# Two matmuls that share a rounded weight, joined into one 512-column matmul, in the MLP and the queries of a two-stack kernel

## The chip, the cores and the metric

The kernel runs on one core of one Trainium2 chip. The metric is the device time of one execution in microseconds. The kernel before takes 3531.47 us, the median of three runs (3530.13 to 3538.19).

## The reference

The reference runs two transformer stacks, two layers each, over 256 tokens of width 1024, in float32. What the change touches are the MLP of each layer of the first stack and the query projection of the expert layer of each layer of the second.

```python
# first stack, each layer l (x: 256 x 1024, mlp_up: 1024 x 4096, mlp_down: 4096 x 1024)
h2 = rms_norm(x, mlp_norm_g[l])
x = x + jnp.square(jax.nn.relu(h2 @ mlp_up[l])) @ mlp_down[l]

# second stack, peer_ffn (w_q: 1024 x 2048)
q = (h @ w_q).astype(f32).reshape(bsz, s, PEER_HEADS, 2, PEER_DKEY // 2)
```

## The kernel before

The kernel is written by hand for each engine: every engine has its own program in a fixed order, and semaphores hold them together. Activations are kept transposed, 128 features on the partitions and the 256 tokens (S) along the free side. A product with a weight matrix is cut into tiles of 128 output features. A tile has one or more units; a unit is eight chunks (KD) of 128x128 weights, 1024 numbers per partition, which SP's queue loads into one of eight slots of a ring (RING).

**Split products.** TensorE multiplies float32 in full in two passes, and numbers rounded to a shorter float (F32R) in one. The kernel splits both operands into a rounded part ("high") and the rounded rest ("low") and adds three products: low weight by high input, high weight by low input and high weight by high input. stream_split does this on TensorE: for each unit three passes of eight 256-column matmuls into the first half of one PSUM bank. Up tiles from number RAW = 3 on (29 of 32 in each layer), all eight down tiles (four units each) and query tiles 3 to 15 go through it. The first three up and query tiles are plain float32, computed before the norm is known (raw_tiles, raw_out).

**The split of a weight.** ScalarE copies a unit from the ring to weight_high (weights_high, line 1961, four slots, three units ahead); VectorE then puts the ring's value minus the high part back into the ring's slot (weights_low, line 2988, two units ahead). Behind every second unit of the MLP VectorE does one add_mod (lines 2966 and 2969, 128x1024), a step of the second stack's modulation vectors. Loads for these steps share SP's queue with the weights.

**An up tile.** TensorE finishes tile j; ScalarE evacuates it with Relu (evac, line 1726), squares it (line 2255) and copies it to up_high (line 2257), each waiting for the one before; VectorE takes the rest, up_low (line 3391). ScalarE's order is: weights_high for tile j, evacuation of j, Square, Copy. VectorE's is: weights_low for tile j, rest of j. In layer 1, VectorE also makes the angles of the second stack's rotary tables before tiles 8 and 14 and their cosines before 12 and 18 (ANGLES, COSINES), and ScalarE their sines before tiles 10 and 16 (SINES). TensorE does 16 small matmuls for modulation sums before tile 22 (UP_SUM, line 1011), and others between down tiles.

**Down and queries.** A down tile is evacuated by ScalarE and added to the residual by VectorE (line 3024); ScalarE squares the result for the next norm. Unit u of the first down tile waits for eight up_low. A query tile is only evacuated, to pq_t. At the first up and query tile, TensorE waits chunk by chunk for hidden_high (ScalarE, line 1948) and for its rest, h_low or second_low (VectorE, split_hidden, line 3001).

Tiles rotate over three banks (BANKS): a tile waits until the one three before it is evacuated.

Of the kernel before, what the change touches and what calls it, by code (L numbers as in the profile page):

```python
# [19 lines left out]
F32 = mybir.dt.float32  # L20
# [155 lines left out]
def two_stacks(nc, io, out):  # L176
    ctx = ExitStack()
    with ctx:
# [14 lines left out]
        def rounded(name, over, first, shape):  # L193

            t = nc.alloc_sbuf_tensor_at(name, shape, F32R, offset=address[over] + 4 * first)
            return t[(slice(None),) * len(shape)]

        arena = sb("arena", [P, 32768])
        ring = sb("ring", [P, RING, 1024])
# [21 lines left out]
        less = rounded("less", "less_plain", 0, [P, P])  # L221
        h_low = rounded("h_low", "hT", 0, [P, KD, S])
        t_high, t_low = rounded("t_high", "hT", 0, [P, KD, S]), rounded("t_low", "ring", 6 * 1024, [P, KD, S])

        PB = [ctx.enter_context(nc.psum_tensor(f"bank{i}", [P, 512], F32)) for i in range(8)]

        def C(name):
# [294 lines left out]
        weight_low = rounded("weight_low", "ring", 0, [P, RING, 1024])  # L522
        hidden_high = rounded("hidden_high", "arena", 25856, [P, KD, S])
        first_weight_high = rounded("first_weight_high", "arena", 0, [P, HIGH, 1024])
        first_high, first_low = rounded("first_high", "uT", 0, [P, KD, S]), rounded("first_low", "arena", 30112, [P, KD, S])
        second_low = rounded("second_low", "arena", 27904, [P, KD, S])
# [15 lines left out]

        up_high = rounded("up_high", "arena", 0, [P, 32, S])
        up_low = rounded("up_low", "arena", 13568, [P, 32, S])

# [233 lines left out]
        gains_m, gains_f = small[:, 24:32], small[:, 32:40]  # L779
        behind_raw = [tiles[label][0] for label in [("conv", RAW)] + [("pq", l, RAW) for l in range(DEPTH)]]  # L780

# [37 lines left out]
        def _(eng):  # L819
# [31 lines left out]

            def stream_split(label, high, low, ready=(None, None), unit_ready=None):

                t, first, count, n = tiles[label]
                assert first == used[0], (label, first, used[0])
                if t + 1 > BANKS:
                    eng.wait_ge(sem("evac"), t + 1 - BANKS)
                for u in range(count):
                    m, k = used[0], units[used[0]][0][1]
                    used[0] += 1  # L860
                    if unit_ready:
                        eng.wait_ge(sem(unit_ready), pe.next(unit_ready, k))
                    eng.wait_ge(sem("weight_low"), split_at[m] + 1)
                    wh = high_of(m)[:, 0:k * P].rearrange("p (k n) -> p k n", n=P)
                    wl = weight_low[:, slot_of[m], 0:k * P].rearrange("p (k n) -> p k n", n=P)
                    for part, (w, x) in enumerate(((wl, high), (wh, low), (wh, high))):
# [448 lines left out]
            def experts(l):  # L1315

                for j in range(RAW, 16):
                    stream_split(("pq", l, j), hidden_high, second_low,
                                 ("hidden_high", "hidden_split") if j == RAW else (None, None))
                for j in range(4):  # L1320
# [285 lines left out]
            for l in range(DEPTH):  # L1606
# [30 lines left out]
                for j in range(RAW, DFF // P):  # L1637
                    if j == UP_SUM:
                        mod_sums(l, 2)
                    stream_split(("up", l, j), hidden_high, h_low,  # L1640
                                 ("hidden_high", "hidden_split") if j == RAW else (None, None))
                def down(m):
                    if m in DOWN_SUMS:
                        mod_sums(l, DOWN_SUMS[m])
                    stream_split(("down", l, m), up_high, up_low, unit_ready=None if m else "up_split")

# [58 lines left out]
        def _(eng):  # L1705
# [259 lines left out]
            def to_residual(name, l, buf, raw=None, gains=None, squares=square_of):  # L1965
# [6 lines left out]
                for m in range(KD):  # L1972
# [4 lines left out]
                    if act.reused("res_add", 4):  # L1977
                        eng.wait_ge(sem("res_add"), act.freed("res_add", 4))
                    evac((name, l, m), buf[:, m % 4, :])
                    if m:  # L1980
# [232 lines left out]
            for l in range(DEPTH):  # L2213
# [32 lines left out]
                for j in range(DFF // P):  # L2246
# [291 lines left out]
        def _(eng):  # L2538
# [78 lines left out]
            def shifted_later(g):  # L2617

                scaled(hT, g, "h_scaled")
                dve.next("h_ready", KD)  # L2620

            def two_norms():
# [390 lines left out]
            def residual(name, l, buf, gain=None):  # L3013
                for m in range(KD):
# [4 lines left out]
                    if name == "down" and m == KD - 1:  # L3019
                        for i in range(MOD_STEPS - 2, MOD_STEPS):  # L3020
                            add_mod(l, i)
                    copied_out((name, l, m))
                    if gain is None:
# [318 lines left out]
            for l in range(DEPTH):  # L3342
# [39 lines left out]
                for j in range(DFF // P):  # L3382
# [15 lines left out]
            for l in range(DEPTH):  # L3398
# [63 lines left out]
```

## Time and profile before

| | before |
|---|---|
| median of three runs | 3531.47 us |
| the three runs | 3530.13, 3531.47, 3538.19 us |
| span of the profiled execution | 3528.6 us |
| TensorE matmul busy | 3419.6 us, 97% |
| TensorE weight load busy | 3075.1 us, 87% |
| VectorE busy | 2454.6 us, 70% |
| ScalarE busy | 1629.3 us, 46% |
| mean granted TensorE clock | 0.988 of full |

The profile comes from an execution whose span, first to last instruction, is 3528.6 us; the time of a run holds some 3 us around that (3531.47 - 3528.6 = 2.9 us). In the rows, PE is TensorE's matmul, PEld its weight load, DVE VectorE, ACT ScalarE. A matmul's duration (283 ns for 256 columns) is longer than the step from one start to the next, because they overlap: the rate is read from start times. L870 is the matmul of stream_split. Names of tensors are the program's; "arena" and "ring" are large buffers that hold many things in turn.

### The profile page before, as it was taken

The numbers are of one execution on the slowest core, as the hardware profiler recorded it, in microseconds if no ns is written. First come the engines' busy times: TensorE is split into PE (matmuls) and PEld (weight loads), VectorE is DVE, ScalarE is ACT, GpSimd is POOL, SyncE is SP. The second block draws the span as 40 slices with busy tenths as digits, with TensorE's granted clock in tenths as the row PEclk, the third lists the DMA queues.
The fourth block names the chain that finished last, engine by engine and source line by source line (L and its number), as shares of the span: only waits on it lengthen the run. The fifth ranks groups of instructions, "written<-read, shape, count | busy, mean of one in ns | idle before, by whom it ended". The sixth has DMA issues, their size and how long they took to land.

```text
span 3528.6 us, 69418 instructions
## 1 busy us (share of the span) xinstructions
PE 3419.6 (97%) x24762; PEld 3075.1 (87%) x24762; DVE 2454.6 (70%) x5088; ACT 1629.3 (46%) x3273; POOL 323.4 (9%) x438
## 2 busy tenths in 40 slices
PE   8999999999999999999999999999899999999998
PEld 7879899988888998889888888888789888888887
DVE  6734456665435756547998888887447998888887
ACT  4143355434434643145555555554345555555554
POOL 0212000020210000000550000000000550000000
PEclk9999999999999999999999999999999999999999
DMA  7633478764336875134348778777254348787775
GB/s 219 182 90 97 116 220 262 229 189 120 84 95 184 262 236 129 49 104 144 92 122 195 193 191 192 190 192 172 63 147 143 91 128 193 190 194 191 192 192 134
DMA packets 644022, 565.20 MB, mean 160 GB/s; under 512 B 62027, under 2 KB 589402, under 8 KB 643546
## 3 DMA queue, kind: packets, MB, share of 16 engines
q1 hardware_dynamic: 638564, 542.16, 58.4%
q0 software_dynamic: 4960, 19.93, 1.7%
q8 instruction: 149, 2.44, 0.3%
q14 instruction: 71, 0.58, 0.1%
q10 hardware_dynamic: 278, 0.08, 0.0%
HBM read 550.52 MB, written 9.44 MB: 159 GB/s over the span
## 4 chain that ended last, share of the span: by engine, by line
PE 90%; DVE 4%; ACT 2%; DMA 1%; issue 1%; POOL 0%; SPq 0%; DVEq 0%; ACTq 0%; POOLq 0%
PE bank L1433 16%; PE bank L870 14%; PE bank L848 14%; PE bank L1453 7%; PE bank L1447 7%; PE bank L1450 7%; PE bank L891 4%; PE bank L1410 3%; PE bank L1385 3%; PE bank L844 2%; PE bank L1395 2%; PE bank L1364 1%; PE bank L1244 1%; PE bank L915 1%; PE bank L959 1%
## 5 line engine op out<-in xcount | busy, mean ns | idle before, releaser
L1433 PE MATMUL bank<-t_high,u_parts 128*128 128x256 f32 x3072 | 431.7, 283 | 5.1 <-DVE u_parts L3278 5.1
L1433 PEld LDWEIGHTS bank<-t_high,u_parts 128*128 128x128 f32 x3072 | 398.4, 188 | 43.3 <-issue 22.4
L3299 DVE TENSOR_TENSOR v_low<-ring,v_high 128x512 fp32r<-128x512 f32 x512 | 337.0, 689 | 62.9 <-ACT v_high L2167 38.3
L1453 PE MATMUL bank<-v_low,w_high 128*128 128x512 f32 x1024 | 323.2, 397 | 0.0
L1447 PE MATMUL bank<-v_high,w_high 128*128 128x512 f32 x1024 | 318.6, 392 | 0.0
L2167 ACT ACTIVATE v_high<-ring 128x512 fp32r<-128x512 f32 x512 | 299.3, 620 | 41.5 <-PE bank L1453 41.5
L1450 PE MATMUL bank<-v_high,w_low 128*128 128x512 f32 x1024 | 315.9, 390 | 0.0
L2370 POOL TENSOR_SCALAR uT<-cst,selT 128x128 f32<-128x128 f32 x256 | 188.2, 744 | 1352.2 <-ACT selT L2092 1347.8
L1726 ACT ACTIVATE arena<-bank 128x256 f32<-128x256 f32 (+1 forms) x270 | 103.8, 387 | 446.4 <-PE bank L848 249.6
L2155 ACT ACTIVATE u_parts<-bank 128x512 fp32r<-128x512 f32 x384 | 217.7, 593 | 194.8 <-DVE bank L3271 193.1
L848 PE MATMUL bank<-hT,ring 128*128 128x256 f32 (+2 forms) x1232 | 283.1, 387 | 9.4 <-DVE hT L2587 5.9
L848 PEld LDWEIGHTS bank<-hT,ring 128*128 128x128 f32 (+2 forms) x1232 | 231.3, 190 | 52.9 <-issue 17.7
L848 PE MATMUL bank<-arena,ring 128*128 128x256 f32 (+2 forms) x1168 | 270.2, 384 | 5.3 <-DVE arena L3010 3.0
L3278 DVE TENSOR_TENSOR u_parts<-bank,u_parts 128x512 fp32r<-128x512 f32 x384 | 246.9, 685 | 12.8 <-ACT u_parts L2155 0.6
L3271 DVE STREAM_TRANSPOSE bank<-ring 128x512 f32<-128x512 f32 x384 | 251.8, 701 | 1.0 <-DMA ring<-in_peer_u 1.0
L848 PEld LDWEIGHTS bank<-arena,ring 128*128 128x128 f32 (+2 forms) x1168 | 217.1, 190 | 40.1 <-DVE arena L3010 3.9
L2178 ACT ACTIVATE w_high<-tab 128x256 fp32r<-128x256 f32 x256 | 107.1, 418 | 280.4 <-DVE tab L3293 280.4
L1450 PEld LDWEIGHTS bank<-v_high,w_low 128*128 128x128 f32 x1024 | 192.3, 188 | 43.1
L1453 PEld LDWEIGHTS bank<-v_low,w_high 128*128 128x128 f32 x1024 | 192.1, 188 | 40.7 <-DVE v_low L3299 0.2
L1433 PE MATMUL bank<-t_low,u_parts 128*128 128x256 f32 x1536 | 214.2, 281 | 0.4
L2988 DVE TENSOR_TENSOR weight_low<-ring,weight_high 128x1024 fp32r<-128x1024 f32 x148 | 179.8, 1221 | 46.4 <-ACT weight_high L1961 45.4
L1447 PEld LDWEIGHTS bank<-v_high,w_high 128*128 128x128 f32 x1024 | 179.1, 188 | 29.7
(455 smaller groups left out, 6434.0 us busy)
## 6 DMA issues: line engine op xcount, KB each, us to landing
ring<-in_peer_v SPq DMA_DIRECT2D x256, 512.0 KB, 4.6
ring<-in_peer_u SPq DMA_DIRECT2D x768, 128.0 KB, 4.3
ring<-in_w_in SPq DMA_DIRECT2D x128, 512.0 KB, 4.0
ring<-in_mlp_up SPq DMA_DIRECT2D x64, 512.0 KB, 4.3
uT<-in_mod_w SPq DMA_DIRECT2D x64, 512.0 KB, 4.9
ring<-in_mlp_down SPq DMA_DIRECT2D x64, 512.0 KB, 4.1
ring<-in_peer_u SPq DMA_DIRECT2D x64, 512.0 KB, 3.8
arena<-in_mod_w POOLq DMA_DIRECT2D x32, 512.0 KB, 4.9
```

Source lines behind the costliest of these rows:

```text
L848: ins = eng.matmul(ps[0:n, 0:width], wv[:, i, :], moving(u * 8 + i), start=(u == 0 and i == 0), stop=(u == count - 1 and i == k - 1))
L870: ins = eng.matmul(PB[t % BANKS][:, 0:S], w[:, i, :], x[:, u * 8 + i, :], start=(u == 0 and part == 0 and i == 0), stop=(u == count - 1 an ...
L1433: ins = eng.matmul(PB[6 + b][:, 0:S], u_parts[:, part, k * P:k * P + P], moving[:, k, :], start=(n == 0), stop=(n == len(products) - 1))
L1447: eng.matmul(PB[2 * tt + q][:, :], w_high[:, b, t], v_high[:, d], start=first, stop=False)
L1450: eng.matmul(PB[2 * tt + q][:, :], w_low[:, b, t], v_high[:, d], start=False, stop=False)
L1453: ins = eng.matmul(PB[2 * tt + q][:, :], w_high[:, b, t], v_low[:, j % 4, d], start=False, stop=last)
L2155: eng.activation(u_parts[:, 0, d], PB[4 + q][:, :], ACT.Copy).then_inc(sem("uH_ready"), 1)
L2167: eng.activation(v_high[:, d], ring[:, 2 + j % 4, d], ACT.Copy).then_inc(sem("vH_ready"), 1)
L2370: ins = ts_(one_p[:, b, j, :], C("iota"), selT[:, 1, at], None, ALU.is_equal)
L3271: eng.transpose(PB[4 + q][:, :].rearrange("p (k e j) -> p k e j", e=QUADS, j=32), blocks_of(f, q)).then_inc(sem("u_turned"), 1)
L3278: tt_(u_parts[:, 1, d], PB[4 + q][:, :], u_parts[:, 0, d].bitcast(F32), ALU.subtract).then_inc(sem("uL_ready"), 1)
L3299: tt_(v_low[:, j % 4, d], ring[:, 2 + j % 4, d], v_high[:, d].bitcast(F32), ALU.subtract).then_inc(sem("vL_ready"), 1)
```

## The change

For a weight chunk, the passes high by low and high by high have the same stationary operand. They become one matmul of 512 columns: its moving operand is two strips of 256 columns, the high and the low input, some way apart in memory (pairs), and its result goes to the two halves of a bank (halves). Low by high stays a 256-column matmul and adds to the first half. In the first unit of a tile the first pair comes before everything else, since it opens the bank.

The two halves have to be added. ScalarE copies the second half to the destination (half_out) and VectorE adds the first to it (both_out). evac now counts up on VectorE for these tiles. For up, Relu can only follow the addition: it is a ScalarE operation of its own, with a wait, before Square. VectorE takes the rest of tile j-1 (up_rest) after both_out of tile j. The gates and the first projections keep their three passes.

```diff
+        def pairs(one, other):
+            apart = other.offset - one.offset
+            return lambda i: bass.AP(one.tensor, (one if apart > 0 else other).offset + S * i,
+                                     [list(one.ap[0]), [abs(apart), 2], [1, S]])
...
+            def pair_products(ps, bank, wh, wl, high, pair, at, k, ready, first, last):
+
+                def from_pair(i):
+                    if ready[1]:
+                        eng.wait_ge(sem(ready[1]), pe.next(ready[1]))
+                    return eng.matmul(halves(bank), wh[:, i, :], pair(at + i), start=(first and i == 0),
+                                      stop=(last and i == k - 1))
+
+                for i in range(k):
+                    if ready[0]:
+                        eng.wait_ge(sem(ready[0]), pe.next(ready[0]))
+                    if first and i == 0:
+                        from_pair(0)
+                    eng.matmul(ps[:, 0:S], wl[:, i, :], high[:, at + i, :], start=False, stop=False)
+                for i in range(1 if first else 0, k):
+                    ins = from_pair(i)
+                return ins
...
+            def half_out(label, dest):
+                t = by_vector(label) - 1
+                eng.wait_ge(sem("unit_done"), last_unit(label))
+                eng.activation(dest, PB[t % BANKS][:, S:2 * S], ACT.Copy).then_inc(sem("half_out"), 1)
...
-                        evac(("pq", l, j), pq_t[:, j, :])
+                        half_out(("pq", l, j), pq_t[:, j, :])
...
-                        evac(("up", l, j), up_t[:, j, :], ACT.Relu)
+                        half_out(("up", l, j), up_t[:, j, :])
                     eng.wait_ge(sem("evac"), tiles[("up", l, j)][0] + 1)
+                    if j >= RAW:
+                        eng.activation(up_t[:, j, :], up_t[:, j, :], ACT.Relu).then_inc(sem("act_step"), 1)
+                        eng.wait_ge(sem("act_step"), act.next("act_step"))
                     eng.activation(up_t[:, j, :], up_t[:, j, :], ACT.Square).then_inc(sem("act_step"), 1)
...
+            def both_out(label, dest):
+                eng.wait_ge(sem("half_out"), dve.next("half_out"))
+                tt_(dest, dest, PB[tiles[label][0] % BANKS][:, 0:S], ALU.add).then_inc(sem("evac"), 1)
...
                     if j >= RAW:
                         weights_low(("up", l, j))
-                    eng.wait_ge(sem("up_high"), dve.next("up_high"))
-                    tt_(up_low[:, j, :], up_t[:, j, :], up_high[:, j, :].bitcast(F32), ALU.subtract).then_inc(sem("up_split"), 1)
+                        both_out(("up", l, j), up_t[:, j, :])
+                    if j:
+                        up_rest(j - 1)
+                up_rest(DFF // P - 1)
...
                 for j in range(RAW, 16):
                     weights_low(("pq", l, j))
+                    both_out(("pq", l, j), pq_t[:, j, :])
```

## Rows read from the trace of the kernel before

**Rows 1.** The page: busy us and instructions by engine; the chain's shares by engine.
```profile
PE 3419.6 (97%) x24762; PEld 3075.1 (87%) x24762; DVE 2454.6 (70%) x5088; ACT 1629.3 (46%) x3273; POOL 323.4 (9%) x438
...
PE 90%; DVE 4%; ACT 2%; DMA 1%; issue 1%; POOL 0%; SPq 0%; DVEq 0%; ACTq 0%; POOLq 0%
```
**Rows 2.** Stretches: us, busy PE, PEld, DVE, ACT, POOL; granted clock, DMA share, GB/s.
```profile
482.00:569.00 87.00, 87.00 (x722) 86.77 (x721) 65.41 (x84) 65.10 (x121) 0.00 (x0) 1.00 0.88 265
...
1558.00:1566.00 8.00, 7.76 (x32) 6.09 (x31) 7.86 (x18) 4.55 (x12) 0.00 (x0) 0.79 0.29 83
```
**Rows 3.** Groups of matmuls by line and shape: count, busy us, mean ns.
```profile
L870 PE MATMUL bank<-up_low,weight_high 128*128 128x256 f32 x512 | 71.9, 283 | 0.0
...
L870 PE MATMUL bank<-h_low,weight_high 128*128 128x256 f32 x464 | 65.1, 283 | 0.0
```
**Rows 4.** Timeline, TensorE, first down unit of layer 0: start us, us, what, count.
```profile
569.07 1.12 PE L870 MATMUL bank<-up_high,weight_low 128*128 128x256 f32 x8
```
**Rows 5.** Timeline, TensorE, two stretches of the expert stage's 512-column matmuls.
```profile
1827.48 0.63 PE L1447 MATMUL bank<-v_high,w_high 128*128 128x512 f32 x2
...
1829.77 0.63 PE L1453 MATMUL bank<-v_low,w_high 128*128 128x512 f32 x2
...
1834.09 0.63 PE L1447 MATMUL bank<-v_high,w_high 128*128 128x512 f32 x2
...
1838.28 0.63 PE L1447 MATMUL bank<-v_high,w_high 128*128 128x512 f32 x2
```
**Rows 6.** Timeline, ScalarE, first up tiles of layer 0.
```profile
488.19 0.36 ACT L1726 ACTIVATE arena<-bank 128x256 f32<-128x256 f32 x1
488.58 0.42 ACT L2255 ACTIVATE arena<-arena 128x256 f32<-128x256 f32 x1
489.03 0.42 ACT L2257 ACTIVATE up_high<-arena 128x256 fp32r<-128x256 f32 x1
489.36 1.04 ACT L1961 ACTIVATE weight_high<-ring 128x1024 fp32r<-128x1024 f32 x1
490.31 0.36 ACT L1726 ACTIVATE arena<-bank 128x256 f32<-128x256 f32 x1
```
**Rows 7.** Groups on VectorE with a bank as operand.
```profile
L2815 DVE TENSOR_TENSOR arena<-arena,bank 128x256 f32<-128x256 f32 x48 | 20.2, 421 | 19.8 <-PE bank L1250 10.3 <-PE bank L1244 8.1
```
**Rows 8.** Timeline, VectorE, layer 1's up part: angles, a lesser weight, an add_mod.
```profile
1147.66 0.35 DVE L2554 TENSOR_SCALAR arena<-wT,cst 128x256 f32<-128x256 f32 x1
...
1150.40 1.23 DVE L2988 TENSOR_TENSOR weight_low<-ring,weight_high 128x1024 fp32r<-128x1024 f32 x1
1151.55 1.28 DVE L2969 SCALAR_TENSOR_TENSOR arena<-uT,cond,arena 128x1024 f32<-128x1024 f32 x1
1152.74 0.42 DVE L3391 TENSOR_TENSOR up_low<-arena,up_high 128x256 fp32r<-128x256 f32 x1
```
**Rows 9.** Timeline, TensorE, last pass of the first split up tile, layer 0.
```profile
485.69 1.12 PE L870 MATMUL bank<-hidden_high,weight_high 128*128 128x256 f32 x8
```
**Rows 10.** Timeline, TensorE, modulation sums before up tile 22.
```profile
538.49 1.84 PE L1011 MATMUL bank<-cst,arena 128*128 128x1 f32 x16
```
**Rows 11.** Timeline, VectorE, the residual add of layer 0's last down tile.
```profile
667.58 0.43 DVE L3024 TENSOR_TENSOR xT<-xT,arena 128x256 f32<-128x256 f32 x1 [3.75 <-ACT arena L1726]
```
**Rows 12.** Timeline, layer 1's up part: table load for sines; a cosine and what follows.
```profile
1153.06 1.28 ACT L1776 ACT_TABLE_LOAD   x1
...
1159.84 0.42 DVE L2568 TENSOR_TENSOR tab<-tab 128x256 f32<-128x256 f32 x1
...
1160.62 1.23 DVE L2988 TENSOR_TENSOR weight_low<-ring,weight_high 128x1024 fp32r<-128x1024 f32 x1
```
**Rows 13.** Timeline, TensorE, behind the last query tile, its wait in brackets.
```profile
1602.85 0.38 PE L1334 MATMUL bank<-arena 128*128 128x128 f32 x1 [0.81 <-ACT arena L1726]
```
**Rows 14.** Timeline, start of the queries: VectorE's split, TensorE's third pass.
```profile
1560.38 2.77 DVE L3001 TENSOR_TENSOR second_low<-hT,hidden_high 128x256 fp32r<-128x256 f32 x8
...
1563.59 1.91 PE L870 MATMUL bank<-hidden_high,weight_high 128*128 128x256 f32 x8
```

More of the change, by code:

```diff
@@ L196, in rounded, with spanning @@
             return t[(slice(None),) * len(shape)]
+        def spanning(name, *places):
+            at = [address[over] + 4 * first for over, first, _ in places]
+            base = min(at)
+            end = max(a + 4 * n * S for a, (_, _, n) in zip(at, places))
+            whole = nc.alloc_sbuf_tensor_at(name, [P, (end - base) // 4], F32R, offset=base)
+            first = [(a - base) // 4 for a in at]
+            return [whole[:, f:f + n * S].rearrange("p (k s) -> p k s", s=S) for f, (_, _, n) in zip(first, places)]
+        def pairs(one, other):
+            apart = other.offset - one.offset
+            return lambda i: bass.AP(one.tensor, (one if apart > 0 else other).offset + S * i,
+                                     [list(one.ap[0]), [abs(apart), 2], [1, S]])
         arena = sb("arena", [P, 32768])
@@ L221, in two_stacks, with halves @@
         less = rounded("less", "less_plain", 0, [P, P])
-        h_low = rounded("h_low", "hT", 0, [P, KD, S])
+        hidden_high, second_low, h_low = spanning("hidden_parts", ("arena", 25856, KD), ("arena", 27904, KD), ("hT", 0, KD))
+        hidden_both, second_both = pairs(hidden_high, h_low), pairs(hidden_high, second_low)
         t_high, t_low = rounded("t_high", "hT", 0, [P, KD, S]), rounded("t_low", "ring", 6 * 1024, [P, KD, S])
         PB = [ctx.enter_context(nc.psum_tensor(f"bank{i}", [P, 512], F32)) for i in range(8)]
+        def halves(bank):
+            return PB[bank][:, 0:2 * S].rearrange("p (a b) -> p a b", b=S)
         def C(name):
@@ L522, in two_stacks @@
         weight_low = rounded("weight_low", "ring", 0, [P, RING, 1024])
-        hidden_high = rounded("hidden_high", "arena", 25856, [P, KD, S])
         first_weight_high = rounded("first_weight_high", "arena", 0, [P, HIGH, 1024])
         first_high, first_low = rounded("first_high", "uT", 0, [P, KD, S]), rounded("first_low", "arena", 30112, [P, KD, S])
-        second_low = rounded("second_low", "arena", 27904, [P, KD, S])
         early_high, early_low = rounded("early_high", "arena", 21760, [P, EARLY_SLOTS, 1024]), rounded("early_low", "ring", 2 * 1024, [P, EARLY_SLOTS + 1, 1024])
@@ L541, in high_of @@
             return (first_weight_high if n in first_units else weight_high)[:, q % HIGH, :]
-        up_high = rounded("up_high", "arena", 0, [P, 32, S])
-        up_low = rounded("up_low", "arena", 13568, [P, 32, S])
+        up_high, up_low = spanning("up_parts", ("arena", 0, 32), ("arena", 13568, 32))
+        up_both = pairs(up_high, up_low)
         mix_t = area(0, KD, S)
@@ L779, in two_stacks @@
         gains_m, gains_f = small[:, 24:32], small[:, 32:40]
-        behind_raw = [tiles[label][0] for label in [("conv", RAW)] + [("pq", l, RAW) for l in range(DEPTH)]]
+        behind_raw = [tiles[label][0] for label in [("conv", RAW)] + [("sub", l, 0) for l in range(DEPTH)]]
         def vector_rows(eng, i, spec, name, src):
@@ L850, in stream, with stream_split @@
                     ins.then_inc(sem("unit_done"), 1)
-            def stream_split(label, high, low, ready=(None, None), unit_ready=None):
+            def stream_split(label, high, low, ready=(None, None), unit_ready=None, pair=None):
                 t, first, count, n = tiles[label]
@@ L865, in stream_split @@
                     wl = weight_low[:, slot_of[m], 0:k * P].rearrange("p (k n) -> p k n", n=P)
+                    if pair is not None:
+                        ins = pair_products(PB[t % BANKS], t % BANKS, wh, wl, high, pair, u * 8, k, ready,
+                                            u == 0, u == count - 1)
+                        ins.then_inc(sem("unit_done"), 1)
+                        continue
                     for part, (w, x) in enumerate(((wl, high), (wh, low), (wh, high))):
@@ L1318, in experts @@
                     stream_split(("pq", l, j), hidden_high, second_low,
-                                 ("hidden_high", "hidden_split") if j == RAW else (None, None))
+                                 ("hidden_high", "hidden_split") if j == RAW else (None, None), pair=second_both)
                 for j in range(4):
@@ L1640, in _ @@
                     stream_split(("up", l, j), hidden_high, h_low,
-                                 ("hidden_high", "hidden_split") if j == RAW else (None, None))
+                                 ("hidden_high", "hidden_split") if j == RAW else (None, None), pair=hidden_both)
                 def down(m):
@@ L1644, in down @@
                         mod_sums(l, DOWN_SUMS[m])
-                    stream_split(("down", l, m), up_high, up_low, unit_ready=None if m else "up_split")
+                    stream_split(("down", l, m), up_high, up_low, unit_ready=None if m else "up_split", pair=up_both)
                 if l == 0:
@@ L1978, in to_residual @@
                         eng.wait_ge(sem("res_add"), act.freed("res_add", 4))
-                    evac((name, l, m), buf[:, m % 4, :])
+                    (half_out if name == "down" else evac)((name, l, m), buf[:, m % 4, :])
                     if m:
@@ L2620, in shifted_later, with up_rest @@
                 dve.next("h_ready", KD)
+            def both_out(label, dest):
+                eng.wait_ge(sem("half_out"), dve.next("half_out"))
+                tt_(dest, dest, PB[tiles[label][0] % BANKS][:, 0:S], ALU.add).then_inc(sem("evac"), 1)
+            def up_rest(j):
+                eng.wait_ge(sem("up_high"), dve.next("up_high"))
+                tt_(up_low[:, j, :], up_t[:, j, :], up_high[:, j, :].bitcast(F32), ALU.subtract).then_inc(sem("up_split"), 1)
             def two_norms():
@@ L3021, in residual @@
                             add_mod(l, i)
+                    if name == "down":
+                        both_out((name, l, m), buf[:, m % 4, :])
                     copied_out((name, l, m))
```

## The prediction

> **What bounds the kernel now.** I read the page first. TensorE is busy 97% of the span, and the chain that ended last is 90% TensorE [rows 1]. So time changes only if TensorE's own stream gets shorter or if TensorE is made to wait. I then read the stage table: in the up part of layer 0's MLP (482 to 569 us) TensorE is busy all the time at full granted clock, and the down part and layer 1 (1130 to 1317 us) look the same, while VectorE and ScalarE are busy three quarters of an up part (65 us each of 87, layer 0) [rows 2]. That is the cover under which the change puts new work, and it is thinner than the average of the page says, because what matters is the serial chain of one tile. The groups of matmuls by line give the counts of one product: 464 in up, 512 in down [rows 3]; the queries have 13 tiles x 8 chunks x 2 layers = 208.
>
> **What TensorE saves.** Of each weight chunk, two 256-column matmuls with the same rounded weight become one of 512 columns. The pairs are 464 in up (29 tiles x 8 x 2 layers), 512 in down and 208 in the queries, 1184 in all. Eight in down take 1.12 us with one of 0.28 at the end: (1.12 - 0.28) / 7 = 120 ns from start to start [rows 4]. No 512-column matmul of this kind runs in these stages. The nearest rows are the expert stage's: from 1834.09 to 1838.28 there are 18 in 4.19 us, 233 ns each, and from 1827.48 to 1829.77 there are 10 in 2.29 us, 229 ns [rows 5]. I take 231 ns, between them. A pair of 240 ns becomes 231 and saves 9 ns; the bounds are 5 ns (235, as far above the 233 as that is above my value) and 13 ns (227, if the 13 ns that 120 has over 256 columns at 2.4 GHz are paid once). Were the two strips of the operand, which lie far apart, read more slowly than one, the saving would be nothing (240). For 1184 pairs: 10.7 us, bounds 6 and 15, and 0 with the slow strips. A tile of up goes from 24 x 120 = 2.88 us to 8 x 120 + 8 x 231 = 2.81 us.
>
> The Trainium skill (TensorE: Matmul & The Clock Gate, Back-to-back issue gap) speaks against this change: it gives an isolated gap of the columns over 2.4 GHz plus about 2.5 ns, so 109 and 216 ns. By it, joining two matmuls would save only 2.5 ns, an estimate of 3 us for all pairs instead of 10.7, and the sum would come near the slower rival below. The rows show 120 ns where it has 109, so the trace does not agree with it.
>
> **What ScalarE and VectorE pay in an up tile.** Before, ScalarE's work for a tile is: a rounded weight, evacuation with Relu, Square, Copy to up_high. In the stretch where it does not wait, that cycle is 488.19 to 490.31 = 2.12 us (0.39 + 0.45 + 0.33 + 0.95) [rows 6]. After, the evacuation is a plain copy of one half; then ScalarE waits for VectorE's both_out, and then comes a Relu of its own. The wait holds up everything behind it in ScalarE's queue, the next rounded weight among it. both_out is a VectorE operation with a bank as operand, 128x256, 421 ns in the nearest row [rows 7]; with some 0.03 us of hand-over it adds 0.45 us. The Relu with its wait adds 0.45 us, as Square to Copy does (488.58 to 489.03) [rows 6]. So the cycle is 2.12 + 0.90 = 3.02 us, against TensorE's 2.81. ScalarE becomes the slower engine by 0.21 us a tile. Before, it had 0.76 us to spare.
>
> VectorE's cycle is a lesser weight (1.15 us from start to start) and in every second tile one add_mod (1.19 us) [rows 8], up_rest and both_out (0.34 each, as eight like them take 2.77 us [rows 14]): 3.02 us in those, 1.83 in the others. It just keeps up with ScalarE in the tiles with an add_mod, and has nothing left there.
>
> **How much of that TensorE feels.** The lesser weight for tile j+3 is made by VectorE after both_out and up_rest of tile j, so 0.40 + 0.34 + 0.34 + 1.22 = 2.3 us after ScalarE began tile j. TensorE wants it two tiles after it ended tile j, 5.6 us. So ScalarE may lag by about 3.2 us before TensorE waits. The waits on banks (a tile needs the one three before it evacuated) come later than that and don't bind. It starts with a lag of 1.4 us: TensorE ends tile 3 at about 486.8, and its evacuation begins at 488.19 [rows 6, 9]. At 0.21 us a tile the room is used up after about nine tiles. Then TensorE loses 0.22 us a tile in tiles 14 to 21 (1.7 us). Before tile 22 it does 1.8 us of small matmuls for the modulation sums [rows 10]; in these ScalarE catches up, and the room lasts until tile 31. At the end the lag meets the change to down: up 31 and the first two units of down wait 0.2 us each, and the third waits 1.7 us, because its lesser weight now stands behind both_out 31 and two up_rest, the last of which waits for the longer chain (2.6 us after ScalarE began instead of 1.7). Sum of the waits in layer 0: 1.7 + 0.6 + 1.7 = 4.0 us. Savings there: 488 pairs x 9 ns = 4.4 us. The last down tile gives its result 0.45 us later, because both_out stands between ScalarE's copy and the residual add, and TensorE then waits for what follows [rows 11]. Layer 0: -4.4 + 4.0 + 0.45 = +0.1 us.
>
> Layer 1 has in its up part the tables for the second block's rotary positions. Two blocks of angles on VectorE take 2.74 us each (1147.66 to 1150.40 [rows 8]) and two cosines 0.78 us each (1159.84 to 1160.62); on ScalarE the sines take 2.0 us with a table load of 1.28 us [rows 12], and 0.8 us the second time, two operations of 0.4. Before, all this lay in spare time. Now each stands in the longest chain: the angles and cosines come at tiles 8, 14, 12 and 18, which all have an add_mod too, and delay both_out by their whole length. Together 2 x 2.74 + 2 x 0.78 + 2.8 = 9.8 us. Layer 1: +0.1 + 9.8 = +9.9 us, of which a little (0.2) is absorbed in the lag at the start: +9.7. Bounds: 4.9 if half of it still finds a gap, 12 if the 512-column matmul is no cheaper.
>
> **Queries.** Here ScalarE does a weight and a copy a tile, VectorE a weight and both_out: far under 2.81 us, so the cover holds. Saving 208 x 9 = 1.9 us. The end costs nothing: 1.9 us of transposes follow before anything reads the last query, and what ends TensorE's wait then is the evacuation of the sub keys [rows 13]. At the start the order changes. TensorE now asks for the first lesser hidden chunk before its second matmul; VectorE starts on these at 1560.38 and takes one in 0.34 us, so TensorE would sit from 1558.5 to 1560.8, then do eight 256-column matmuls and follow VectorE with the pairs to about 1563.6. Before, a third pass followed until 1565.30, at 213 ns a matmul [rows 14], half the clock (1.2 GHz; the granted clock of 1558 to 1566 was 0.79 [rows 2]). So up to 1.7 us are won at each of the two starts, or nothing if the longer idle time makes the low clock fall on the pairs or the tiles behind. I take 0.9 each, 1.8 together. Loads: SP's queue holds weight loads behind loads that wait on add_mod; these may come 3 to 6 us later. A slot of the ring is loaded eight units ahead and rounded three ahead, 5 x 2.8 = 14 us, so I cost this at nothing; it would cost the excess if the lag passed that.
>
> **Sum.** +0.1 + 9.7 - 1.9 - 1.8 = +6.1 us on a profiled execution with a span of 3528.6 us. The runs shown are 3530.13 to 3538.19 with a median of 3531.47, 2.9 us above the span; that part does not change. 3531.5 + 6.1 = 3537.6 us. ScalarE's chain in up takes back what the wider matmuls give.
>
> **Rivals.**
> - The cover holds (0.20). If ScalarE's tile cycle is under 2.81 us, or the wait for both_out overlaps with something, all pairs count: -10.7 - 1.8 + 0.9 (two down ends) = -11.6, so 3519.9; with 227 ns, 3515. For it: ScalarE was busy only 65 of 87 us. Against it: its steps of one tile depend on one another and the next weight stands behind them.
> - Slower (0.27): the 512-column matmul costs as much as two (240 ns), because its operand is two strips; in effect the change then doesn't do what it says. Savings fall to nothing, and as a tile then takes 2.88 us the lag grows by 0.14 us a tile and the waits of layer 0 shrink from 4.0 to 1.8 us: 1.8 + 0.45 = +2.3 in layer 0, 9.6 more in layer 1, 0 in the queries and at their starts: +14.2, 3545.7. For it: the 1.7 % by which the expert stage's 512-column rows differ among themselves shows that the place of an operand counts. Against it: all of them are under 240. It decides from about 233 ns on (each ns costs 0.7 us: +6.1 becomes +7.1 at 232.5).
> - Only the layer 1 tables are better hidden (0.10): +1 us, 3532.5.
>
> **How the numbers follow.** The forecast, 3537.6, has 0.43; its own range is 3532 to 3543, cut nearly in the middle by the bound of +0.2% (3538.5). A measurement of this kernel can tell about 0.2%, 7 us, from no change. Slower by over that: 0.20 of the forecast's 0.43 and all of the slower rival's 0.27: 0.47. Faster by over that: the cover rival, 0.17 of its 0.20. Same: 0.36. The range, 3519 to 3547, takes in all cases.
>
> **What would show it.** Matmuls from pairs starting 227 to 235 ns apart. ScalarE's up cycle 3.0 us with no idle time on TensorE's account; idle time of TensorE ended by weight_low (VectorE) of about 4 us in layer 0 and 14 us in layer 1, the latter mostly between 1150 and 1190. The up part of layer 0 as long as before, that of layer 1 some 10 us longer, both down parts some 2 us shorter. I am wrong if TensorE does not idle in up, or if pairs come at 240 ns.

## The result, and the profile after

| | before | changed |
|---|---|---|
| median, beside each other | 3530.08 us (8 runs) | 3540.26 us (8 runs, 3536.41 to 3546.86) |
| ratio | | 1.0025, 95% interval 1.0015 to 1.0035 |
| span of the profiled execution | 3528.6 us | 3538.1 us |

The change makes the kernel slower by a quarter of a per cent: 8.8 us by the ratio (5.3 to 12.4 us). The two medians lie 10.2 us apart, inside that interval. The forecast was 3537.6 us within 3519 to 3547, +0.17% on the runs shown then.

The page of the changed kernel, busy time by engine and the chain, answers to [rows 1]:

```profile
PE 3417.0 (97%) x23578; PEld 3015.1 (85%) x23578; DVE 2490.7 (70%) x5188; ACT 1647.5 (47%) x3331; POOL 323.9 (9%) x438
...
PE 85%; DVE 8%; ACT 4%; issue 1%; DMA 1%; POOL 0%; SPq 0%; DVEq 0%; ACTq 0%; POOLq 0%
```

TensorE has 1184 matmuls and weight loads fewer. Its share of the ending chain fell from 90 to 85%, VectorE's doubled. The stretches of the changed kernel (columns as in [rows 2]) show where:

```profile
482.00:569.00 87.00, 87.00 (x489) 73.59 (x488) 70.65 (x109) 70.90 (x145) 0.00 (x0) 1.00 0.92 259
569.00:667.00 98.00, 96.52 (x560) 84.49 (x560) 66.53 (x71) 40.37 (x55) 0.00 (x0) 1.00 0.81 239
1130.00:1217.00 87.00, 79.83 (x435) 68.68 (x434) 69.97 (x116) 66.03 (x135) 0.00 (x0) 0.96 0.82 233
1217.00:1317.00 100.00, 97.88 (x557) 85.37 (x556) 67.29 (x78) 50.29 (x78) 0.00 (x0) 0.98 0.81 245
```

The first and third lines are the up parts of layers 0 and 1, the others their down parts. Layer 0's up part still looks full. Layer 1's has TensorE busy 79.8 of 87 us, while VectorE and ScalarE, whose chain of steps sets the pace there (below), are busy only 70 and 66: an engine that bounds a stage by a chain of dependent steps does not look busy.

**The matmuls.** Timeline of TensorE in down, layer 0: start, us, count. L904 is the 512-column matmul of a pair, L912 the 256-column one of low by high.

```profile
571.38 1.11 PE L912 MATMUL bank<-up_parts,weight_low 128*128 128x256 f32 x8
572.32 1.77 PE L904 MATMUL bank<-up_parts,weight_high 128*128 128x512 f32 x7
...
574.10 1.18 PE L912 MATMUL bank<-up_parts,weight_low 128*128 128x256 f32 x8
```

Seven pairs (the record of the eighth is missing) take 1.77 us with one of 0.39 at the end: 1.38 / 6 = 230 ns from start to start. The eight 256-column matmuls before them step at (1.11 - 0.28) / 7 = 119 ns, where they stepped at 120 [rows 4]. So a pair saves 11 ns in all; the lengths of parts below say the same (experiment 6: 2.8 us for the 256 pairs of a down part). I count it as a pair of 229 ns against 240. No matmul with one contiguous strip stands beside it; against the expert stage's 229 to 233 ns [rows 5] the two strips show no cost.

**The chain of a tile.** Timeline of ScalarE and VectorE in layer 0's up part, the stretch that answers to [rows 6]; L1781 is half_out, L2676 both_out, L2304 the Relu, L2306 the Square, L2308 the Copy, L2009 the next rounded weight.

```profile
493.01 0.36 ACT L1781 ACTIVATE arena<-bank 128x256 f32<-128x256 f32 x1
493.41 0.42 DVE L2676 TENSOR_TENSOR arena<-arena,bank 128x256 f32<-128x256 f32 x1
...
493.87 0.42 ACT L2304 ACTIVATE arena<-arena 128x256 f32<-128x256 f32 x1 [0.49 <-DVE arena L2676]
...
494.31 0.42 ACT L2306 ACTIVATE arena<-arena 128x256 f32<-128x256 f32 x1
494.77 0.42 ACT L2308 ACTIVATE up_parts<-arena 128x256 fp32r<-128x256 f32 x1
495.09 1.04 ACT L2009 ACTIVATE weight_high<-ring 128x1024 fp32r<-128x1024 f32 x1
...
496.04 0.36 ACT L1781 ACTIVATE arena<-bank 128x256 f32<-128x256 f32 x1
```

From one half_out to the next ScalarE takes 3.03 us and doesn't wait for TensorE; its only wait is the 0.49 us for both_out. TensorE's tile takes 8 x 0.120 + 8 x 0.229 = 2.79 us when nothing holds it up.

**Where TensorE waits.** Timeline of TensorE, layer 1's up part and the change to down (last line), the lines with a wait in brackets:

```profile
1155.13 0.75 PE L904 MATMUL bank<-hidden_parts,weight_high 128*128 128x512 f32 x1 [1.97 <-DVE weight_low L3049]
...
1166.35 0.47 PE L904 MATMUL bank<-hidden_parts,weight_high 128*128 128x512 f32 x1 [1.05 <-DVE weight_low L3049]
...
1170.16 0.47 PE L904 MATMUL bank<-hidden_parts,weight_high 128*128 128x512 f32 x1 [0.77 <-DVE weight_low L3049]
...
1178.93 0.66 PE L904 MATMUL bank<-hidden_parts,weight_high 128*128 128x512 f32 x1 [2.75 <-DVE weight_low L3049]
...
1192.54 0.47 PE L904 MATMUL bank<-hidden_parts,weight_high 128*128 128x512 f32 x1 [0.64 <-DVE weight_low L3049]
...
1236.44 1.52 PE L912 MATMUL bank<-up_parts,weight_low 128*128 128x256 f32 x8 [2.09 <-DVE weight_low L3049]
```

Every one of them ends with a lesser weight of VectorE (L3049). In layer 0 there is one such wait, of 1.48 us, in down at 578.60. Waits of 0.2 us a tile don't appear as idle time, since a matmul's duration overlaps the next start; so I measure a part by its length. The lengths below are taken from the start times, from the first to the last matmul of the part that the change touches; MLP 0 is the up and down part of layer 0, and so on. The column "sum" is the difference to the kernel before.

| us | MLP 0 | MLP 1 | queries 0 | queries 1 | sum | as ratio | measured ratio |
|---|---|---|---|---|---|---|---|
| before | 183.2 | 185.9 | 41.4 | 41.6 | | | |
| changed | 182.6 | 196.3 | 37.7 | 36.2 | +7.0 | 1.0020 | 1.0025 |
| 1 tables in down | 182.6 | 185.4 | 37.8 | 36.2 | -3.9 | 0.9989 | 0.9994 |
| 2 weight before the wait | 177.9 | 184.6 | 36.2 | 36.2 | -11.0 | 0.9969 | 0.9979 |
| 3 both | 177.9 | 180.1 | 36.2 | 36.2 | -15.5 | 0.9956 | 0.9951 |
| 4 no Relu | 177.9 | 187.7 | 37.7 | 36.2 | -6.3 | 0.9982 | 0.9988 |
| 5 each pair as two | 185.2 | 197.4 | 37.3 | 37.3 | +10.9 | 1.0031 | 1.0043 |
| 6 up as before | 180.4 | 183.1 | 37.7 | 36.2 | -8.4 | 0.9976 | 0.9963 |
| 7 both, again | 177.9 | 180.1 | 37.7 | 36.2 | -14.0 | 0.9960 | 0.9962 |

The sum is the four differences to before, plus what the lengths leave out. In front of the queries of each layer it is 2.4 us: TensorE now idles 2.13 us there, and the matmul before no longer overlaps the next. Behind the queries it is 0.6 us: from the last start to the next matmul that waits are 3.48 us, where they were 2.87. Behind MLP 0 and MLP 1 it is 0.2 and 0.1 us, up to the first matmul on the new norm's output (6.49 against 6.30 and 14.96 against 14.86 us). In experiment 5, whose parts end on 256-column matmuls, it is 0.1 us less behind each part. Where a part's code is the same its length repeats within 0.1 us, but for the first queries, which depend on the clock.

The rest of the difference of the two profiled spans, 2.5 of 9.5 us, lies in parts whose code is the same: at the first up matmul the changed kernel is already 1.8 us behind (485.39 against 483.60). Between profiled executions such parts differ more than that: against the kernel before they are together from 3.9 us shorter (experiment 6) to 10.2 us longer (experiment 3). Half of the latter goes with the granted clock of one stretch. Between MLP 1 and the queries lies a stretch that the change doesn't touch, but for the wait at its end; stretches of the kernel before and of experiment 3, columns as in [rows 2]:

```profile
1318.00:1558.00 240.00, 226.53 (x1547) 195.94 (x1546) 130.76 (x291) 73.17 (x168) 1.19 (x2) 0.93 0.35 93
...
1307.00:1555.00 248.00, 235.51 (x1553) 203.29 (x1551) 133.50 (x296) 76.21 (x176) 1.19 (x2) 0.90 0.35 92
```

Up to the wait it is 5.0 us longer at a granted clock of 0.90 instead of 0.93. Why the clock was lower there is open. The measured ratios scatter around those of the sums by about 0.1%.

### The profile page after: what moved, and what is told of

Same layout as the page of the kernel before. It is cut to its first block, busy times and chain, and to the rows that moved or that the text cites. A ratio compares the mean times of both kernels' runs of the same rounds, so it can differ in the third digit from the quotient of the medians.

```text
span 3538.1 us, 67212 instructions
## 1 busy us (share of the span) xinstructions
PE 3417.0 (97%) x23578; PEld 3015.1 (85%) x23578; DVE 2490.7 (70%) x5188; ACT 1647.5 (47%) x3331; POOL 323.9 (9%) x438
## 4 chain that ended last, share of the span: by engine, by line
PE 85%; DVE 8%; ACT 4%; issue 1%; DMA 1%; POOL 0%; SPq 0%; DVEq 0%; ACTq 0%; POOLq 0%
PE bank L1475 16%; PE bank L867 14%; PE bank L1495 7%; PE bank L1489 7%; PE bank L1492 7%; PE bank L904 5%; PE bank L933 4%; PE bank L1452 3%; PE bank L1427 3%; PE bank L912 2%; PE bank L894 2%; PE bank L863 2%; PE bank L1437 2%; PE bank L1406 1%; PE bank L1286 1%
## 5 line engine op out<-in xcount | busy, mean ns | idle before, releaser
L2215 ACT ACTIVATE v_high<-ring 128x512 fp32r<-128x512 f32 x512 | 299.4, 621 | 41.6 <-PE bank L1495 41.6
L1768 ACT ACTIVATE arena<-bank 128x256 f32<-128x256 f32 (+1 forms) x170 | 65.6, 391 | 314.9 <-PE bank L867 250.0
L1475 PEld LDWEIGHTS bank<-t_low,u_parts 128*128 128x128 f32 x1536 | 195.9, 188 | 1.2 <-DVE t_low L3378 1.2
```

The source lines that it names most:

```text
L1475: ins = eng.matmul(PB[6 + b][:, 0:S], u_parts[:, part, k * P:k * P + P], moving[:, k, :], start=(n == 0), stop=(n == len(products) - 1))
L2215: eng.activation(v_high[:, d], ring[:, 2 + j % 4, d], ACT.Copy).then_inc(sem("vH_ready"), 1)
```

## The experiments

**1. The rotary tables out of the up part.** Theory: ScalarE's serial chain of one up tile bounds up, and work that used to fit beside TensorE now adds to the chain. Rivals: VectorE itself, with one more operation, is the slow engine; or the wider matmuls slow other traffic.

```diff
-        ANGLES, SINES, COSINES = (8, 14), (10, 16), (12, 18)
+        ANGLES, SINES, COSINES = (1, 2), (2, 3), (3, 4)
...
                     if name == "down":
                         weights_high((name, l, m))
+                    if name == "down" and l == 1 and m in SINES:
+                        sines(SINES.index(m))
...
+                    if name == "down" and l == 1 and m in COSINES:
+                        cosine(COSINES.index(m))
+                    if name == "down" and l == 1 and m in ANGLES:
+                        i = ANGLES.index(m)
+                        angles(i, ("moba", "mla")[i], 2 + i, 1)
                     if name == "down":
                         both_out((name, l, m), buf[:, m % 4, :])
```

> The changed kernel with layer 1's rotary tables (angles and cosines on VectorE, sines on ScalarE) moved from its up part to its down part, into places where both engines wait for TensorE. Theory (the serial chain of one up tile, 3.02 us against TensorE's 2.79, has no room for them): layer 1's MLP is about 9.8 us shorter than in the changed kernel and takes the same time as layer 0's relative to the kernel before; some 3530.5 us in all, ratio to before about 1.000. Rival (VectorE or memory traffic is slowed by the wider matmuls, wherever the tables stand): under 3 us shorter, 3537 to 3540.

Measured: 3529.22 us (10 runs), ratio to before 0.9994 (0.9984 to 1.0003). MLP 1 is 10.9 us shorter than in the changed kernel, and nothing else in the table changed. The tables cost that much only where they stood: 9.4 us of it lie in up (95.1 to 85.7 us from its first matmul to down's first), 1.5 us in down, which had met a low clock (below). The table of waits of that kernel around MLP 1 (engine, line, waited for: us, times, longest) has one at the change to down and one of code that the change doesn't touch, at 1121.24, ahead of the up part:

```profile
PE bank L912 <- DVE weight_low L3049: 2.1, 1, 2.1
PE bank L957 <- ACT arena L1801: 0.5, 1, 0.5
```

**2. The next weight before the wait.** Only ScalarE's order changes; VectorE does the same operations in the same order.

```diff
-                        weights_high(("up", l, j))
+                        if j == RAW:
+                            weights_high(("up", l, j))
                         half_out(("up", l, j), up_t[:, j, :])
+                        if j + 1 < DFF // P:
+                            weights_high(("up", l, j + 1))
```

> The changed kernel with one thing reordered on ScalarE in the up part: the next tile's rounded weight is made right after half_out, before the wait for both_out; VectorE's work and order are the same. Theory (ScalarE's wait is what is long): ScalarE's cycle falls from 3.02 to about 2.5 us, TensorE's waits in layer 0's MLP go from 1.5 us in one plus small ones to none (-4.5 us), in layer 1 most of 14 us go (-9.8), since the lag of a table is won back in the next tiles: about 3526 us, ratio 0.999. Rival (VectorE, with one more addition per tile, is the slow engine): no change, 3540.

Measured: 3522.94 us (10 runs), ratio 0.9979 (0.9970 to 0.9989). MLP 0 is 4.7 us shorter than in the changed kernel, MLP 1 11.7. Timeline of ScalarE, layer 0, up (L2307 is the Relu here, L2309 the Square, L2311 the Copy):

```profile
521.93 0.38 ACT L1781 ACTIVATE arena<-bank 128x256 f32<-128x256 f32 x1 [0.26 <-PE bank L904]
522.22 1.05 ACT L2009 ACTIVATE weight_high<-ring 128x1024 fp32r<-128x1024 f32 x1
523.16 0.41 ACT L2307 ACTIVATE arena<-arena 128x256 f32<-128x256 f32 x1
523.60 0.42 ACT L2309 ACTIVATE arena<-arena 128x256 f32<-128x256 f32 x1
524.05 0.42 ACT L2311 ACTIVATE up_parts<-arena 128x256 fp32r<-128x256 f32 x1
524.73 0.39 ACT L1781 ACTIVATE arena<-bank 128x256 f32<-128x256 f32 x1 [0.26 <-PE bank L904]
```

The cycle is 2.80 us, and what ends it is TensorE again: the weight fills the time in which VectorE adds, and the Relu does not wait at all. This rules VectorE out as the bound of layer 0, since its work is unchanged. In layer 1 TensorE still waits 2.8 us in three places for a lesser weight, and MLP 1 is 4.5 us longer than with the tables moved as well (experiment 3):

```profile
PE bank L904 <- DVE weight_low L3052: 2.8, 3, 1.8
```

**3. Both.** The edits of experiments 1 and 2 together.

> Both edits together: tables in the down part and the rounded weight before the wait. Theory: no wait for a lesser weight is left in either MLP; each MLP is 4.9 us shorter than in the kernel before (5.4 us from 488 pairs at 11 ns, less 0.45 at its end), the queries 3 us together: 3521 to 3522 us, 18.9 us under the changed kernel, ratio to before 0.9975. Rival (half of the loss lies elsewhere): 3530 or more.

Measured: 3517.03 us (5 runs), ratio 0.9951 (0.9937 to 0.9966). The MLPs are 5.3 and 5.9 us shorter than before, and no wait for a weight is left in them. The ratio is lower than the 0.9975 expected, mostly because the expectation was summed wrongly. Its own terms, 2 x 4.9 and 3 us, make 12.8 us under the kernel before, a ratio of 0.9964, which the interval holds; 0.9975 came from taking 18.9 us off the changed kernel's median, which lies further above before than its parts do. By parts the profiled execution gives 15.5 us. In it neither start of the queries fell into the low clock, so the queries gave 4.7 us together instead of 3, and layer 1's MLP gave 0.9 more than 4.9. That execution was all the same the longest of the five (3525.09 us): its untouched parts were 10.2 us longer than in the kernel before, half of it in the stretch shown above. So its parts don't explain the median.

**4. The chain one link shorter.** From the changed kernel, the Relu of the split up tiles is left out; this kernel squares the plain sum and so computes something else.

```diff
-                    if j >= RAW:
-                        eng.activation(up_t[:, j, :], up_t[:, j, :], ACT.Relu).then_inc(sem("act_step"), 1)
-                        eng.wait_ge(sem("act_step"), act.next("act_step"))
```

> The changed kernel without the Relu of the up tiles from number 3 on, so the square is of the plain sum: this leaves out part of the computation, to price one link of the chain. Theory: ScalarE's cycle falls by 0.45 us to 2.57, under TensorE's 2.79; layer 0 loses its 4.5 us of waits, layer 1 about 7 of its 14: some 11.5 us less than the changed kernel, about 3529 us. Rival (VectorE's 3.02 us in every second tile is the bound): under 2 us, 3538 to 3540.

Measured: 3529.34 us (10 runs), ratio 0.9988 (0.9979 to 0.9998). MLP 0 is 177.9 us, the same as with the weight first: taking 0.45 us of work from the chain or filling its 0.49 us of wait gives the same, because either brings it under 2.79. MLP 1 is 8.6 us shorter than in the changed kernel and 7.6 us longer than with both edits: here the tables still don't fit. VectorE's 3.02 us in every second tile, a figure of the prediction, did no harm by itself in layer 0.

**5. The matmul's own price.** Each pair but a tile's first as two matmuls of 256 columns, one for each half of the bank.

```diff
-                    return eng.matmul(halves(bank), wh[:, i, :], pair(at + i), start=(first and i == 0),
-                                      stop=(last and i == k - 1))
+                    if first and i == 0:
+                        return eng.matmul(halves(bank), wh[:, i, :], pair(at + i), start=True, stop=False)
+                    both = pair(at + i)
+                    for half in range(2):
+                        ins = eng.matmul(PB[bank][:, S * half:S * half + S], wh[:, i, :],
+                                         bass.AP(both.tensor, both.offset + half * both.ap[1][0], [list(both.ap[0]), [1, S]]),
+                                         start=False, stop=bool(last and i == k - 1 and half))
+                    return ins
```

> The changed kernel with each 512-column matmul issued as two of 256 columns into the two halves of the bank (the first pair of a tile stays one, since it opens the bank); the copies, the additions and all orders stay. This prices the matmul by itself. Theory: a pair costs 240 ns again instead of 229, 11 ns for each of 1084 pairs = 11.9 us of TensorE's time, but ScalarE's chain of 3.02 us in up hides part: each MLP is 2.7 us longer than in the changed kernel (all in down: 256 pairs x 11 ns = 2.8 us), the queries 2 us together: +7 us, about 3546 to 3547. Rival (TensorE's stream sets the up part too): +12 us, 3552.

Measured: 3544.29 us (4 runs), ratio to before 1.0043 (1.0027 to 1.0060). By the two ratios to before that is 0.18% or 6.4 us over the changed kernel. Timeline of TensorE, down, layer 0:

```profile
602.09 1.12 PE L918 MATMUL bank<-up_parts,weight_low 128*128 128x256 f32 x8
603.05 1.12 PE L908 MATMUL bank<-up_parts,weight_high 128*128 128x256 f32 x8
```

Every matmul of 256 columns has its 120 ns again ((1.12 - 0.28) / 7; the second line shows the first eight of 16). MLP 0 is 2.6 us longer than in the changed kernel. Down loses 2.4 of it, for 248 split pairs, where 248 x 11 ns are 2.7; up, with 203 split pairs worth 2.2 us, loses only 0.2 (85.7 to 85.8 us). So in the changed kernel ScalarE and not TensorE sets layer 0's up part. MLP 1 is only 1.1 us longer, 0.6 in up and 0.5 in down; in down the changed kernel had lost 1.5 us to a low clock (below), and this one had not. The parts make 3.9 us over the changed kernel, where 7 were expected.

**6. The change without the up part.** Up has its three passes and evacuation with Relu; down and queries are as in the changed kernel.

```diff
-                        half_out(("up", l, j), up_t[:, j, :])
+                        evac(("up", l, j), up_t[:, j, :], ACT.Relu)
...
-                        both_out(("up", l, j), up_t[:, j, :])
-                    if j:
-                        up_rest(j - 1)
-                up_rest(DFF // P - 1)
+                    up_rest(j)
```

> The change made only in down and the queries; the up part has its three passes and its evacuation with Relu on ScalarE as in the kernel before. Theory (all the loss is in the up part's chain): no waits in up, down saves 2.8 us a layer less 0.45 at its end, the queries 3 us together: 7.7 us under the kernel before, ratio 0.998. Rival (the additions in down and the queries cost too): ratio 1.000 or more.

Measured: 3518.11 us (5 runs), ratio 0.9963 (0.9950 to 0.9976), lower than the 0.998 expected. Both MLPs are 2.8 us shorter than before, as 256 pairs x 11 ns say. So the additions in down and the queries have their cover, but for the 0.1 to 0.6 us behind each part. The parts give 8.4 us, 0.9976, at the edge of the interval; for what the median has beyond that the runs show no cause but the spread of the untouched parts, which were 3.9 us shorter in this profiled execution than in that of the kernel before.

**7. Both edits once more, beside these two.**

> The kernel of both edits once more, beside the other two on one chip: ratio to before 0.995 to 0.9975, and 2 to 8 us under the kernel that has the change only in down and the queries, since the up parts save 232 pairs x 11 ns = 2.6 us each.

Measured: 3517.57 us (5 runs), ratio 0.9962 (0.9948 to 0.9975). The MLPs have the lengths of experiment 3 to 0.1 us (177.9 and 180.1). Stretches of this kernel:

```profile
482.00:569.00 87.00, 87.00 (x504) 76.83 (x503) 74.60 (x114) 75.11 (x154) 0.00 (x0) 1.00 0.90 274
...
1120.00:1210.00 90.00, 90.00 (x519) 79.49 (x518) 77.95 (x122) 77.19 (x159) 0.00 (x0) 1.00 0.90 273
```

TensorE is full in both up parts, and the two others are busier than in the kernel that waited for them. Against experiment 6 the median is 0.5 us lower, where 2 to 8 us were expected and the MLPs' lengths say 5.6; whole-kernel times of five runs each, spread over 7 us, don't resolve that. Still it is a version that beats both kernels given, the one before by about 0.4%.

## Why the prediction was right, point by point

- **The price of the wide matmul** was 231 ns with bounds 227 and 235; it steps at 230, and with the ns that its neighbours gain it counts as 229. The slower rival needed 240 and is out. The rule of the Trainium skill (TensorE: Matmul & The Clock Gate, Back-to-back issue gap) that would have left 2.5 ns of saving does not agree with the traces: 240 against 229.
- **ScalarE's cycle** was to be 3.02 us and is 3.03. Experiments 2 and 4 shorten it in two ways and both remove layer 0's waits; that its wait, not VectorE's added work, is the cause is shown by experiment 2. This mechanism carries the forecast, and it held.
- **Layer 0**: waits of 4.0 us forecast (1.9 in up, 2.1 at the change to down), 4.7 measured (182.6 - 177.9: 2.7 in up, 2.0 in down). The savings were to be 4.4 us and are 5.3. The last evacuation costs 0.2 us, not 0.45. MLP 0 with it is 0.4 us shorter, where +0.1 was forecast. Near nothing in sum, as said.
- **Signs that failed.** "Both down parts some 2 us shorter" did not come: they are 0.8 us shorter in layer 0 (97.7 to 96.9) and 1.3 us longer in layer 1 (99.9 to 101.3). By the prediction's own terms it should have said 0.2 us: 2.3 us saved, less the 2.1 of waits that it had put there. And the profile shows 1.5 and 9.3 us of idle time ended by weight_low, not 4 and 14; in the lengths TensorE loses 4.7 and 16.2 us against experiment 3 (182.6 and 196.3 against 177.9 and 180.1).
- **Layer 1's tables** were to cost 9.8 us, and in up they cost 9.4 (experiment 1). MLP 1 with its last evacuation is 10.5 us longer than before, against 9.7 forecast. The term that was missing is the granted clock. Three times after a wait TensorE ran at 1.2 GHz for most of 4 us, twice in up and once in down. Down is 1.5 us longer for it than in experiment 1; what the two in up cost, beside ScalarE's lag, was not measured apart. Stretches of the changed kernel:

```profile
1155.00:1159.00 4.00, 3.87 (x14) 3.51 (x15) 2.98 (x4) 2.39 (x5) 0.00 (x0) 0.57 0.38 96
...
1179.00:1183.00 4.00, 4.00 (x15) 3.52 (x16) 2.88 (x5) 2.46 (x5) 0.00 (x0) 0.57 0.49 135
...
1237.00:1241.00 4.00, 4.00 (x16) 3.33 (x15) 4.00 (x5) 0.00 (x0) 0.00 (x0) 0.57 0.52 155
```

  TensorE had waited 2.09 us before the last one. The same unit's two rows of matmuls last 1.52 and 3.26 us there, against 1.19 and 2.00 with the tables in down, where a wait of 2.08 us was followed by the full clock. So a wait of 2 us costs another 1.5 us at times.
- **Start of the queries**: TensorE waits 2.13 us for the first lesser chunk, as said, and the gain depends on the clock. Timeline of the changed kernel, both layers:

```profile
1573.78 0.47 PE L904 MATMUL bank<-hidden_parts,weight_high 128*128 128x512 f32 x1 [2.13 <-DVE hidden_parts L3062]
1574.09 1.19 PE L912 MATMUL bank<-hidden_parts,weight_low 128*128 128x256 f32 x8
1575.08 3.54 PE L904 MATMUL bank<-hidden_parts,weight_high 128*128 128x512 f32 x8
...
2631.31 0.47 PE L904 MATMUL bank<-hidden_parts,weight_high 128*128 128x512 f32 x1 [2.13 <-DVE hidden_parts L3062]
2631.62 1.12 PE L912 MATMUL bank<-hidden_parts,weight_low 128*128 128x256 f32 x8
2632.58 2.00 PE L904 MATMUL bank<-hidden_parts,weight_high 128*128 128x512 f32 x8
```

  In layer 0 the pairs fell into the low clock (3.54 us), in layer 1 they did not (2.00). With 1.1 us saved by the 104 pairs of a layer and 0.6 lost at the end, the two starts gave 0.1 and 1.9 us. The 0.9 us for each was a middle of nothing and 1.7, and one start of each kind came: that the sum fits is luck. Whether a first pass of low by high, before the wait, would be better was not tried.
- **End of the queries** was costed at nothing. This step failed, by 0.6 us in each layer. The last sub-key evacuation does end TensorE's wait, but it starts later. Changed kernel (PEld is TensorE's weight load):

```profile
1611.76 2.44 PE L1368 MATMUL bank<-cst,ring 128*128 128x128 f32 x16
...
1612.84 0.42 PEld L1368 LDWEIGHTS bank<-cst,ring 128*128 128x128 f32 x4 [0.29 <-DVE arena L2676]
1612.88 2.06 ACT L1768 ACTIVATE arena<-bank 128x512 f32<-128x512 f32 x4 [0.55 <-PE bank L1368]
1613.53 0.42 PEld L1368 LDWEIGHTS bank<-cst,ring 128*128 128x128 f32 x4 [0.27 <-ACT arena L1768]
...
1615.00 2.16 PE L1376 MATMUL bank<-arena 128*128 128x128 f32 x17 [0.81 <-ACT arena L1768]
```

  From the first transpose to the matmul behind them are 3.24 us; before, they were 1600.09 to 1602.85, 2.76 us [rows 13]. The four sets of transposes now take 2.44 us, where they took 1.94, for two waits: the third set waits 0.29 us for a bank until VectorE has added the last query tile (L2676), and the fourth 0.27 us until ScalarE has emptied the first set's bank (L1768). ScalarE starts on that only after the same addition: evac has a wait for it at this tile (behind_raw in the kernel, which the change moved from the first split query tile to the first sub-key tile). The row names the transposes for its 0.55 us, but VectorE's addition ran from 1612.37 to 1612.79. No run tested this link by itself. I had read who ended the wait and not what that one waited for.
- **The sum** was +6.1 us. By the parts, with what the lengths leave out, it is -0.4 (MLP 0), +10.5 (MLP 1), -0.7 and -2.4 (queries 0 and 1): +7.0. The forecast terms were +0.1, +9.7 and -3.7 for both queries, so MLP 0 and MLP 1 were off by -0.5 and +0.8 and the queries by +0.6: their pairs gave 0.4 us more and the starts 0.2 more than said, and the two ends took 1.2. The whole kernel says 8.8 us (ratio 1.0025, so 5.3 to 12.4). I had put most chance on slower by over 0.2%, though the number itself stood just inside that bound. The range of 3519 to 3547 us took in every rival; that the time lies in it shows little; what speaks for the prediction is the cycle of 3.02 us, the tables and a value 2.7 us from the median.

## What to carry to other kernels

Where two engines share the evacuation of a tile, the round trip lies in the first engine's queue; put independent work for the next tile between the hand-over and the wait. Here that one reordering turned 1.0025 into 0.9979. Judge cover by the longest chain of one tile against the bound engine's time for it, not by busy shares; once the chain is longer than the tile, side work beside it is paid nearly in full (here 9.4 us of tables that had been free, and 1.5 us more by the clock after a wait). And when a copy is delayed at the end of a stage, follow the banks through the next stage before costing it at nothing.

## What the runs showed of the hardware

- A 512-column matmul of rounded float whose operand is two strips far apart steps at 230 ns, two of 256 columns with the same weights at 240.
- A wait of TensorE of 2 us is sometimes followed by most of 4 us at 1.2 GHz and sometimes not (2.09 and 2.08 us before the same unit), which makes one wait's price uncertain by 1.5 us.
- The MLP parts of the same code repeat to 0.1 us between kernels while whole executions of one kernel spread over some 10 us, so lengths of parts resolve what the median can't.
- A stretch of untouched code took 5.0 us more in one execution than in another, at a granted clock of 0.90 instead of 0.93.
